# A two-block transformer in one launch: a query projection, a factor spread and the angle arithmetic of the first block moved

## What is computed

```python
xn = _rms_norm(x, attn_norm[l])
h = xn @ w_in[l]                      # three families of attention from one product
q_a = _rms_norm(c_q @ mla_w_uq[l])    # MLA: 6 heads, 96 wide, rope on the last 32
k_a, v_a = c_kv @ mla_w_ukv[l], k_rope
o_a = softmax(q_a @ k_a) @ v_a
a = p[:, :, 0] - lam * p[:, :, 1]     # differential: 4 heads with two maps each
o_b = _rms_norm(a @ v_b, diff_out_gain[l]) * (1.0 - lambda_init)
o_c = softmax(q_c @ k_c) @ v_c        # grouped-query: 6 heads
x = x + concat([o_a, o_b, o_c]) @ w_o[l]
gate, up = jnp.split(_rms_norm(x, ffn_norm[l]) @ w_gate_up[l], 2, axis=-1)
x = x + (jax.nn.silu(gate) * up) @ w_down[l]
```

## Time and profile before

| | before |
|---|---|
| median of three runs | 1671.51 us (1669.98 to 1673.21) |
| the profiled execution's own time | 1670.88 us |
| its span | 1669.1 us |
| TensorE busy | 1629.8 us, 98% of the span |
| VectorE busy | 1209.8 us, 72% |
| ScalarE busy | 899.5 us, 54% |
| mean granted TensorE clock | 0.994 of full speed |

### The profile page before, as it was taken

One profiled execution on the slowest core, in us unless ns is written; L12 is line 12 of the kernel. 1 busy time (PEld: TensorE's weight loads), 2 busy tenths in 40 slices (PEclk: granted clock), 3 DMA queues, 4 the chain that ended last, 5 costly groups with the idle time before them and its releaser, 6 DMA issues.

```text
span 1669.1 us, 31856 instructions
## 1 busy us (share of the span) xinstructions
PE 1629.8 (98%) x13566; PEld 1578.4 (95%) x13566; DVE 1209.8 (72%) x1785; ACT 899.5 (54%) x1378; POOL 116.3 (7%) x72
## 2 busy tenths in 40 slices
PE   9988999999999999999999999999999999999997
PEld 9977999999879999999999989999999999899997
DVE  5887777647976776487858768984777767679963
ACT  5585644454775444544544665554545546655542
POOL 2020000020110000210000110001100001010000
PEclk9999999999999999999999999999999999999999
DMA  8313556553225655565345535655464454446560
GB/s 294 107 65 106 198 191 200 179 193 129 95 60 190 217 190 188 193 213 198 112 152 176 167 118 173 217 174 176 149 221 163 141 161 166 152 137 205 184 208 33
DMA packets 53598, 275.03 MB, mean 165 GB/s; under 512 B 6480, under 2 KB 7376, under 8 KB 53328
## 3 DMA queue, kind: packets, MB, share of 16 engines
q1 hardware_dynamic: 53312, 271.94, 48.1%
q10 hardware_dynamic: 144, 1.05, 0.2%
HBM read 271.13 MB, written 1.05 MB: 163 GB/s over the span
## 4 chain that ended last, share of the span: by engine, by line
PE 81%; DVE 13%; ACT 3%; issue 2%; DMA 0%; SPq 0%; ACTq 0%; DVEq 0%
PE bank L809 17%; PE bank L811 17%; PE bank L812 17%; PE scores L809 3%; PE scores L811 3%; PE scores L812 3%; DVE weights_lo L650 3%; DVE x_lo L958 2%; PE heads L809 2%; PE heads L811 2%; PE heads L812 2%; ACT probs L1229 1%; PE heads L1967 1%; PE scores L818 1%; DVE x L2426 1%
## 5 line engine op out<-in xcount | busy, mean ns | idle before, releaser
L650 DVE TENSOR_TENSOR weights_lo<-raw,weights_hi 128x1536 fp32r<-128x1536 f32 (+2 forms) x344 | 583.0, 1712 | 221.6 <-ACT weights_hi L639 220.9
L639 ACT ACTIVATE weights_hi<-raw 128x1536 fp32r<-128x1536 f32 (+5 forms) x352 | 500.2, 1440 | 173.0 <-PE bank L812 74.5
L809 PE MATMUL bank<-x_hi,weights_lo 128*128 128x256 f32 (+1 forms) x1556 | 433.8, 279 | 0.3 <-DVE weights_lo L650 0.3
L811 PE MATMUL bank<-x_lo,weights_hi 128*128 128x256 f32 (+1 forms) x1556 | 430.9, 277 | 0.0
L812 PE MATMUL bank<-x_hi,weights_hi 128*128 128x256 f32 (+1 forms) x1556 | 430.8, 277 | 0.0
L809 PEld LDWEIGHTS bank<-x_hi,weights_lo 128*128 128x128 f32 (+1 forms) x1556 | 290.6, 187 | 3.5 <-issue 2.7
L811 PEld LDWEIGHTS bank<-x_lo,weights_hi 128*128 128x128 f32 (+1 forms) x1556 | 290.8, 187 | 0.1
L812 PEld LDWEIGHTS bank<-x_hi,weights_hi 128*128 128x128 f32 (+1 forms) x1556 | 290.8, 187 | 0.0
L809 PE MATMUL bank<-hidden_hi,weights_lo 128*128 128x256 f32 x692 | 191.5, 277 | 2.0 <-DVE hidden_lo L2278 2.0
L811 PE MATMUL bank<-hidden_lo,weights_hi 128*128 128x256 f32 x692 | 191.0, 276 | 0.0
L812 PE MATMUL bank<-hidden_hi,weights_hi 128*128 128x256 f32 x692 | 191.0, 276 | 0.0
(11 more groups left out here) (427 smaller groups left out, 3487.3 us busy)
## 6 DMA issues: line engine op xcount, KB each, us to landing
raw<-in_w_b SPq DMA_DIRECT2D x202, 768.0 KB, 4.3
raw<-in_w_a SPq DMA_DIRECT2D x120, 768.0 KB, 4.3
raw<-in_w_a SPq DMA_DIRECT2D x16, 512.0 KB, 3.6
raw<-in_w_a SPq DMA_DIRECT2D x2, 736.0 KB, 8.4
raw<-in_w_a SPq DMA_DIRECT2D x2, 672.0 KB, 6.9
x<-in_x SPq DMA_DIRECT2D x2, 512.0 KB, 5.2
mem<-in_mem ACTq DMA_DIRECT2D x1, 1024.0 KB, 8.3
raw<-in_w_b SPq DMA_DIRECT2D x2, 512.0 KB, 5.4
```

The source lines that it names most:

```text
L639: nc.scalar.activation(whi[c % SPLIT][:, 0:n], raw[c % RAW][:, 0:n], ACT.Copy).then_inc(*s.mark("weights_hi", c))
L650: nc.vector.tensor_tensor(wlo[c % SPLIT][:, 0:n], raw[c % RAW][:, 0:n], whi[c % SPLIT][:, 0:n].bitcast(F32), ALU.subtract).then_inc(*s.mar ...
L809: ins = nc.tensor.matmul(dst, wl, xh, start=start, stop=False, skip_group_check=skip)
L811: nc.tensor.matmul(dst, wh, xl, start=False, stop=False, skip_group_check=skip)
```

## The change

It makes three moves. In the attention of both layers the job `uq2` goes from behind step 4 to behind step 5, between the flips of `uk2` and `uq0`, and its `rope` from step 5 to step 6. `dif_spread` goes from inside step 7, ahead of `pair_out`, to behind it. And the 13 angle operations of layer 0, which stood in one block behind step 8, are dealt out: two of them behind `lam_sum` early in the layer, the other eleven in groups of 2, 2, 3, 2 and 2 behind the rounds 3 to 7 of the feed-forward.

```diff
-        order_a += [("latent", 0), ("job", "dk0"), ("rope", "dq0"), ("spread", "latent"), ("lam_sum", 0), ("rope", "kv"), ("job", "g0"), ("flip", "dq0"),
+        order_a += [("latent", 0), ("job", "dk0"), ("rope", "dq0"), ("spread", "latent"), ("lam_sum", 0), ("angles", 0), ("rope", "kv"), ("job", "g0"), ("flip", "dq0"),
...
-                  4: [("rope", "uq0"), ("rope", "uq1")], 5: [("rope", "uq2")], 6: [("roots", "uq")], 7: [("dif_spread", 0)],
+                  4: [("rope", "uq0"), ("rope", "uq1")], 6: [("rope", "uq2"), ("roots", "uq")],
                   12: [("root_table", "o"), ("job", "o3")]}
...
-                 4: [("job", "uq2"), ("flip", "uk0")], 5: [("flip", "uk1"), ("flip", "uk2"), ("flip", "uq0")],
-                 6: [("dif_sum", 0), ("flip", "uq1"), ("flip", "uq2"), ("chunks", 19)], 7: [("dif_out", 0)],
-                 8: [("angles", 0), ("job", "part0")], 9: [("job", "part1")], 10: [("job", "part2")]}
+                 4: [("flip", "uk0")], 5: [("flip", "uk1"), ("flip", "uk2"), ("job", "uq2"), ("flip", "uq0")],
+                 6: [("dif_sum", 0), ("flip", "uq1"), ("flip", "uq2"), ("chunks", 19)], 7: [("dif_spread", 0), ("dif_out", 0)],
+                 8: [("job", "part0")], 9: [("job", "part1")], 10: [("job", "part2")]}
...
             order_a += [("job", f"gate{i}"), ("ffn_hi", i - 2), ("ffn_in", i - 1), ("job", f"up{i}"), ("ffn_lo", i - 2), ("ffn_out", i - 1)]
+            order_a += [("angles", i - 2)] if 3 <= i < 8 else []
...
-                        vector_angles(dve)
+                        vector_angles(dve, name)
...
-        def vector_angles(dve):
+        def vector_angles(dve, part):
...
+            if part == 0:
+                dve.wait_ge(loaded["pos"], 16)
+                nc.vector.tensor_copy(ANG[:, :], POS[:, :]).then_inc(*O.mark("angle", 0))
+                dve.wait_ge(*O.at(0, "angle", 0))
+                nc.vector.tensor_scalar(ANG[:, :], ANG[:, :], const("inv_freq"), None, ALU.mult).then_inc(*O.mark("angle", 1))
+            elif part == 1:
...
+            elif part == 3:
+                for n in (1, 2, 3):
+                    dve.wait_ge(*O.at(0, "angle", 1 + n))
+                    nc.vector.scalar_tensor_tensor(out=ANG[:, :], in0=TURNS[:, :], scalar=-pieces[n], in1=ANG[:, :], op0=ALU.mult, op1=ALU.add)\
+                      .then_inc(*O.mark("angle", 2 + n))
```

53 lines of the change are left out of this document (26 added, 27 removed).

## The result

The changed kernel takes 1675.3 us (median; 1671.14 to 1678.22 us over 20 runs), the kernel before 1671.39 us in the same comparison (1669.36 to 1675.45, 20 runs). The ratio is 1.0021, 95% interval 1.0015 to 1.0027: 3.9 us more by the medians, 2.5 to 4.5 us by the interval. The forecast was 1673.9 us, +2.4 us against the profiled execution, in a range of 1670.0 to 1677.2 us. So the change makes the kernel slightly slower, by more than the forecast had it and just above the 3.3 us that the prediction called measurable.

What follows compares the result with a forecast made beforehand. TensorE (98% busy) bounds it, with a ring through three engines in attention. -4.27 + 0.7 + 0 + 5.4 + 0.6 = +2.4 us on 1670.88 gives 1673.3; medians lie 0.6 higher: 1673.9 us, range 1670.0 to 1677.2.

Steps and rivals of the forecast that it cites:

- The angles leave the attention: In layer 0's attention, removing the block of angles saves its 2.82 us wait and what comes after: -4.27 us.
- The first part returns early: Layer 0, ahead of the grouped-query values: the conversion and first multiplication add 0.7 us, bounds 0 and 0.7.
- The other eleven in the feed-forward: Eleven angle operations in feed-forward rounds 3 to 7 cost nothing; up to 4.1 us if the cover failed.
- `uq2` a pair later: Pairs 4 to 8: the flip of `uq0` waits for ScalarE, delaying pair 6's scores 1.9 us, its exponentials 1.65 us.
- The spread behind the values: Ahead of pair 8's maxima, VectorE's two multiplications add 1.2 us; 0.15 us is spare at pair 9's transposes.
- The clock: TensorE idle ahead of pair 4's transposes may drop to half clock: 0 to 1.2 us a layer, 0.6 taken in all.
- the first: Clock falls in both layers ahead of pair 4, and again ahead of pair 8's scores: 1676.7 us, chance 0.20.
- The spread stays hidden: Pair 8's maxima still find slack before pair 9, so 1.2 us a layer fall out: 1671.5 us, chance 0.14.
- It fills the idle time and wins: Product and later spread take the place of 0.78 and 0.98 us idle, nothing given back: 1664.4 us, chance 0.08.
- The angles aren't hidden: In the feed-forward the angles cost up to 4.1 us on top, up to 1678.0 us; chance 0.06.
- the distance between the layers: Sign: layers 0 and 1 lie about 345.5 us apart both before and behind the attention.

Runs made afterwards that it cites:

- the run with both moves: Kernel after with the angles left in the attention as before, so late `uq2` and late spread together: 1680.36 us, ratio 1.0050.
- the one with six and six: Kernel after with six products of zeros in each of two TensorE waits, ahead of pair 5's scores and pair 4's transposes: 1673.34 us, ratio 1.0017.

## Why the prediction was nearly right

By its own steps:

- **The angles leave the attention (-4.27 us): right in size, wrong in what it is made of.** 4.12 us by the distances of the run with the angles alone. But the clock at 145 us was worth 0.3 us of it, by two profiles without that fall. "This holds the wait of 2.82 us and what comes after it" should have been VectorE's 4.85 us in front of pair 9, less the 1.0 us for which it would have waited there anyway.
- **The first part returns early (+0.7): 0.47 us measured**, between the bounds. The 0.71 us of the prediction run to the start of a third angle operation. What counts is how much later the values start behind the copy in front of them: 0.66 us in the kernel after (51.88 and 52.54 us), 0.19 before (51.80 and 51.99 us). The 0.39 us by the Trainium skill ("VectorE: DVE Perf Modes", the section on the TRN2 errata) come nearer to this delay than the 0.71, though they are less than the two rows' own durations, 0.28 + 0.35 us.
- **The other eleven in the feed-forward (0): right.** TensorE 64.00 us busy of 64.
- **`uq2` a pair later (+1.65 a layer): right in place and path, 1.79 us in size.** Without a fall of the clock the scores of pair 6 come 2.04 us later against pair 4 (1.9 forecast); the flip of `uq0` waits 0.82 us for ScalarE's copy, in the rows of the run with both moves and of the one with six and six. What TensorE no longer waited ahead of GpSimd's factor came back ahead of the scores of pair 8: 1.47 us idle where 1.7 was forecast.
- **The spread behind the values (+1.2, of which 0.15 hidden): 1.19 us a layer**, by itself and on top of `uq2`. The 0.15 us that the prediction took off as slack were none, as the run with the spread alone shows. The two moves together cost 2.98 us a layer where the prediction had 2.7.
- **The clock (+0.6 in the whole, bounds 0 and 1.2 a layer): the step that was mis-sized.** It measured 1.0 us a layer on average over six layers, 2.0 in the whole. Single layers go from 0 to 1.81 us, beyond the upper bound. The prediction took one number, 1.7 us a fall, and hid 0.5 of it; a fall there comes in two lengths, of 3.4 and 6.8 us, and costs 0.9 or 1.6 to 1.8 us. It also took less than the middle of its bounds, although it had named the 2.18 us of activity ahead of the known fall as the row that spoke for a fall in both layers.
- **Sum.** -4.12 + 0.47 + 2 x 2.98 + 2.0 = +4.3 us, beside 3.9 measured by the medians, 3.5 by the ratio (2.5 to 4.5), and 2.4 forecast. The falls of the clock behind the latents are left out, since nothing in the change bears on them.

Of the rivals, the first came nearest: its 1676.7 us and the forecast of 1673.9 lie equally far from the 1675.3 measured. The clock did fall ahead of pair 4 in both layers of the profile after. Its second fall, ahead of the scores of pair 8, is in none of the six layers. "The spread stays hidden" and "It fills the idle time and wins" fall with the runs that made each move alone, and "The angles aren't hidden" with the feed-forward window.

The sign that the prediction gave for itself, the distance between the layers, failed, and that shows a flaw in how it was chosen: 345.5 us was expected, 343.69 us stands at the transposes of pair 4 and 342.98 us at the first product of the next norm. They agree with each other within 0.7 us, the difference of the two layers' stretches at half clock. But both are lower than forecast. The 347.05 and 342.78 us of before held a fall of 6.8 us at 384 us, 3.1 us of time, that had nothing to do with the attention and was absent after. Another 0.7 us lie between the next norm of layer 0 and the sums of layer 1 (209.34 us after, 210.00 before); their cause wasn't looked for. A single distance over a stretch that can hold such a fall can be off by 3 us.

## What to carry to other kernels

A product that fills idle time keeps the clock up as well: before moving it away, read what TensorE has left to do in the stretch, and price a fall both by its length and by whether TensorE is the bound behind it (3.4 us at half clock cost 1.5 us behind the latents, 0.3 us behind the angles and 0.9 us ahead of pair 4). An idle row that vanishes is no gain when the engines form a ring; follow the delay to the next exponentials first. Compare distances inside a stage over several profiles, and not whole spans, when falls of the clock come by chance.

## What the hardware showed that was not expected

- The same program at the same place sometimes dropped its clock and sometimes did not: ahead of pair 4 not at all, for 3.4 us or for 6.8 us; behind the narrow sums in 9 of 11 profiles. It makes two profiles of one kernel differ by up to 3.1 us at one place; how much of the spread of all runs it explains was not measured.
- Ten fp32 products 2 columns wide took as long as ten of 128 columns (2.18 us to the next product either way, at full clock), but only with the narrow ones did the clock come down, in 14 layers of 22 against none of 6. TensorE stood still in neither.
- Products of zeros count as activity: twelve rows in 1.50 us and twelve in 1.60 kept the clock at 1.00 in both layers.
